# A fused decoder step: raw transposes of the first rows, their scale applied later, and the first weights in quarters

## The chip, the cores and the metric

One NeuronCore of one Trainium2 chip runs the whole program. The metric is the device time of one execution in microseconds (us); lower is better. The kernel before was timed three times: 1256.57, 1258.19 and 1259.11 us, median 1258.19 us.

## What is computed

One layer of a decoder on 264 rows of 1024 features (256 prompt rows, 8 decode rows), everything in float32. The part that the change touches is the start:

```python
def rms_norm(x, g):
    xf = x.astype(jnp.float32)
    y = xf * lax.rsqrt(jnp.mean(xf * xf, axis=-1, keepdims=True) + EPS)
    return (y * g.astype(jnp.float32)).astype(x.dtype)

parts = jnp.split(rms_norm(x, norm_attn) @ w_in, cuts, axis=-1)   # D_MODEL 1024 -> 4888 columns
q_a, k_c, v_c, k_s, v_s, k_w, v_w, g_nsa, q_b, k_b, v_b, g_mrg = parts
```

Then come QK-norm and rotary of queries and keys, a compression of cached and new keys and values (two small MLPs with GELU), two attentions (NSA and MoBA, for prompt and decode rows), a gated merge through `w_up_a`, `w_up_b` and `w_out`, and a mixture of 32 experts of 1024 x 2048 and 1024 x 1024 weights (12 MiB each, about 403 MB in all).

## The kernel before, in words

Every engine has its own instruction list, written out by hand in the order in which it runs; semaphores (`wait_ge`, `then_inc`) tie them together. There is no planner. All loads of weights go through SyncE's one DMA queue, in program order; some cache pages go through ScalarE's queue.

**The start.** SyncE (lines 2163 to 2179) issues, in this order: the first 128 prompt rows `x[:, 0]` (512 KB), the identity (64), the gains (4), the first half (4 of 8 chunks of 128 rows) of projection block 0 of `w_in` (1024), the second 128 prompt rows (512), the 8 decode rows (32), the second half of block 0 (1024), block 1 (1120), seven small gain vectors (32 each), the rest of the constants (1174), the page table, the four small loads of `small_weights` (line 494), and then blocks 2 to 5 (2048 KB each). `small_weights` begins with `sp.wait_ge(n_sq, 3)`: its destinations lie on ScalarE's `square_out`, so it waits until ScalarE has squared all three row tiles.

For each row tile i, ScalarE squares the rows with a running sum (line 2327) and takes the root (2329), VectorE takes the reciprocal (2428) and multiplies the rows by it (2429), TensorE transposes the scaled rows in eight pieces into a PSUM bank pair (`turn_x`, 2232), and ScalarE (2336) and VectorE (2437) copy the transposed rows out into `xnT`, times the feature gain. TensorE starts with eight matmuls on zeros (2227) while the first data comes.

**The projection.** `project(n)` (2243) runs blocks n = 0 to 5 of `w_in`: for each of the two prompt tiles eight chunk products of 128 x 512 into one bank, then the decode rows as 128 x 32 products. ScalarE's `evacuate(n)` (2339) copies each bank out and squares it for the QK-norm. Block 0 is special: `turn_x(1)` stands in the middle of its first tile and `turn_x(2)` after it. SyncE then issues, in order, its share of the compressed-cache pages (`cached`, 2152: 32 DMAs), the two 2 MB weights of the compression, stores of new keys, the key pages of three caches (`load_item` of items 8 to 10), and the stores and reloads of `q_rows` (2200 to 2204), by which the decode queries go out to HBM and come back on all partitions. VectorE's `moba_scores` (L985, L987) needs these.

**After the projection.** TensorE transposes the cached rows, runs the compression's hidden layer (L635), packs the result (`packed`, L687) and goes on to attention, where `gate_tile(f)` (L698) reads `xnT` again for the merge gates. `packed(1)` waits for the last GELU piece, which VectorE (L994 to L1006) and ScalarE (L888) make between and behind the eight `moba_scores`. GpSimd (`compress_pool`, 557) clears buffers. Then come the merge and the experts, whose weights stream through nine slots; a slot is loaded again as soon as its matmuls are done.

Of the kernel before, what the change touches and what calls it, by code (L numbers as in the profile page):

```python
# [26 lines left out]
P = 128  # L27
# [94 lines left out]
def build(nc, t, const_at, const_w):  # L122
    ctx = ExitStack()
    with ctx:
# [151 lines left out]
        x_in, gain_in, n_root, n_scaled, n_turned = [sem(f"n_x{i}") for i in range(NT)], sem("n_gain"), sem("n_root"), sem("n_scaled"), sem("n_turned")  # L276
        n_sq, n_kept, n_clear = sem("n_sq"), [sem(f"n_kept{i}") for i in range(NT)], sem("n_clear")
# [104 lines left out]
        cmp_read, cmp_ready, cmp_T, cmp_kept = sem("cmp_read"), sem("cmp_ready"), sem("cmp_T"), sem("cmp_kept")  # L382
# [4 lines left out]
        early, early_in = [at(out_at, 2 * D), at(d_at, 2 * D)], sem("early_in")  # L387
        extra, extra_in = at(extra_at, SLOT), x_in[1]
        odd_first, odd_second, odd_last = at(k_at, SLOT), at(d_at + KC * TOK, 3 * D), at(m_at + 2 * D, D)
# [25 lines left out]
        def landing(slot):  # L415
            base = dense_count[slot] if slot < RING else 16 if slot == EXTRA else 0
            return (early_in if slot == EARLY else extra_in if slot == EXTRA else ring_in[slot]), base, 16 * len(slot_runs(slot))
# [139 lines left out]
        def compress_pool(pool):  # L557
            pool.wait_ge(rope_done, 5)
            for i in range(2):
                nc.gpsimd.memset(rT[i][:, 18, :], 0.0).then_inc(n_clear, 1)  # L560
            pool.wait_ge(p_turned, 11)
# [129 lines left out]
        def gate_tile(pe, f):  # L691
            if f % 4 == 0:
# [8 lines left out]
        def attend_pe(pe):  # L701
# [66 lines left out]
            def unit_values(u):  # L768
# [3 lines left out]
                if u == 0:  # L772
                    pe.wait_ge(cmp_kept, 1)
# [1386 lines left out]
        with nc.Block() as block:  # L2160
            @block.sync
            def _(sp):
# [4 lines left out]
                sp.dma_start(first[:, 0:KC // 2, :], source[:, 0:KC // 2, :]).then_inc(half_in, 16)  # L2167
                sp.dma_start(x[:, 1, :], t["x_prompt"][0, P:2 * P, :]).then_inc(x_in[1], 16)
                sp.dma_start(x[0:DB, 2, :], t["x_sample"].rearrange("a b d -> (a b) d")).then_inc(x_in[2], 16)
                sp.dma_start(first[:, KC // 2:KC, :], source[:, KC // 2:KC, :]).then_inc(ring_in[0], 16)  # L2170
# [52 lines left out]
            def _(pe):  # L2223
                zeros = xdT.rearrange("p c b -> p (c b)")
                pe.wait_ge(n_clear, 2)
                for _ in range(8):
# [5 lines left out]
                def turn_x(i):  # L2232
                    r = ROWS[i]
                    pe.wait_ge(n_scaled, i + 1)
# [8 lines left out]
                def project(n, between=None):  # L2243
# [6 lines left out]
                    for i in range(2):  # L2250
# [11 lines left out]
                        for c in range(KC):  # L2262
                            if n == 0 and i == 0 and c == KC // 2:
                                turn_x(1)
                                pe.wait_ge(ring_in[0], landed[0])
                            mm = nc.tensor.matmul(out, xnT[:, c, P * i:P * i + P], columns(c), start=(c == 0), stop=(c == KC - 1))  # L2266
                        mm.then_inc(proj_done, 1)
                        if n == 0 and i == 0:
                            turn_x(2)
# [44 lines left out]
                project(V_B, lambda: turn(K_B))  # L2314
                compress_pe(pe)
# [5 lines left out]
            def _(act):  # L2321
                act.wait_ge(n_clear, 1)
                nc.scalar.activation(small[:, 12:13], eps, ACT.Sqrt)
                for i in range(NT):
# [3 lines left out]
                    act.wait_ge(n_sq, i + 1)  # L2328
                    nc.scalar.activation(rstd[0:r, i:i + 1], sumsq[0:r, i:i + 1], ACT.Sqrt, scale=1.0 / D, bias=eps[0:r, :]).then_inc(n_root, 1)
                    if i == 0:  # L2330
# [206 lines left out]
```

## Time and profile before

| | |
|---|---|
| median of three runs | 1258.19 us (1256.57 to 1259.11) |
| profiled execution, its own time | 1257.01 us |
| its span (first to last instruction) | 1255.1 us, 16432 instructions |
| busy: PE, DVE, ACT, POOL | 1214.9 us (97%), 379.0 (30%), 194.5 (15%), 16.1 (1%) |
| HBM read | 459.54 MB, 370 GB/s over the span |
| chain that ended last, shares | PE 58%, DMA 29%, SPq 8%, DVE 3%, issue 1% |
| DMA in 40 slices, GB/s, slices 1 to 12 | 326 187 245 240 213 200 126 161 347 308 233 419 |
| DMA, slices 13 to 39 | 424 to 431 |

PE is TensorE, DVE VectorE, ACT ScalarE, POOL GpSimd, SPq the issuing of DMAs by SyncE. A slice is 31.4 us. The span is cut short by 1.9 us against the execution's own time; differences in the span are differences in the time. In the chain, "SPq" is the time in which SyncE was issuing DMAs and nothing else is seen to have held up what came after.

### The profile page before, as it was taken

The numbers are of one execution on the slowest core, as the hardware profiler recorded it, in microseconds if no ns is written. First come the engines' busy times: TensorE is split into PE (matmuls) and PEld (weight loads), VectorE is DVE, ScalarE is ACT, GpSimd is POOL, SyncE is SP. The second block draws the span as 40 slices with busy tenths as digits, with TensorE's granted clock in tenths as the row PEclk, the third lists the DMA queues.
The fourth block names the chain that finished last, engine by engine and source line by source line (L and its number), as shares of the span: only waits on it lengthen the run. The fifth ranks groups of instructions, "written<-read, shape, count | busy, mean of one in ns | idle before, by whom it ended". The sixth has DMA issues, their size and how long they took to land.

```text
span 1255.1 us, 16432 instructions
## 1 busy us (share of the span) xinstructions
PE 1214.9 (97%) x6431; PEld 552.2 (44%) x6431; DVE 379.0 (30%) x931; ACT 194.5 (15%) x440; POOL 16.1 (1%) x28
## 2 busy tenths in 40 slices
PE   9999999999999999999999899999999898999998
PEld 5556777685533433334333232343334333333332
DVE  2545865324533221222222121321222121221223
ACT  3223244202301100010100001110010100000011
POOL 0000000011000000000000000000000000000000
PEclk9999999999999999999999999999999999999999
DMA  9787563598699999999999999999999999999995
GB/s 326 187 245 240 213 200 126 161 347 308 233 419 431 426 424 429 427 426 427 427 426 427 427 428 426 426 428 426 425 426 428 428 426 427 427 426 428 426 427 244
DMA packets 81067, 463.58 MB, mean 369 GB/s; under 512 B 20290, under 2 KB 35418, under 8 KB 55906
## 3 DMA queue, kind: packets, MB, share of 16 engines
q1 hardware_dynamic: 76386, 461.51, 90.8%
q10 hardware_dynamic: 4608, 1.05, 0.5%
q8 instruction: 52, 0.85, 0.3%
q14 instruction: 21, 0.17, 0.0%
HBM read 459.54 MB, written 5.09 MB: 370 GB/s over the span
## 4 chain that ended last, share of the span: by engine, by line
PE 58%; DMA 29%; SPq 8%; DVE 3%; issue 1%; ACT 0%; DVEq 0%
PE banks L1301 21%; DMA arena<-w_down 18%; PE banks L1381 10%; DMA arena<-w_gu 10%; PE banks L698 5%; PE banks L1278 3%; PE banks L1238 2%; PE banks L875 2%; PE banks L1567 2%; SPq L2157 2%; SPq L238 1%; PE banks L1259 1%; PE banks L1331 1%; SPq L265 1%; PE banks L1287 1%
## 5 line engine op out<-in xcount | busy, mean ns | idle before, releaser
L1301 PE MATMUL banks<-arena 128*64 128x512 f32 x1984 | 440.6, 594 | 19.3 <-DMA arena<-w_gu 18.4
L1301 PEld LDWEIGHTS banks<-arena 128*64 128x64 f32 x1984 | 134.8, 136 | 294.1 <-issue 248.8
L1381 PE MATMUL banks<-arena 128*64 128x512 f32 x992 | 221.2, 593 | 4.2 <-DMA arena<-w_down 3.8
L1481 DVE TENSOR_SCALAR arena<-banks 128x512 f32<-128x512 f32 x32 | 22.1, 692 | 373.3 <-PE banks L1301 352.9
L1381 PEld LDWEIGHTS banks<-arena 128*64 128x64 f32 x992 | 69.5, 137 | 137.3 <-issue 117.1
L1437 ACT ACTIVATE arena<-arena 128x512 f32<-128x512 f32 x32 | 20.2, 630 | 524.8 <-DVE arena L1481 524.8
L2266 PE MATMUL banks<-arena 128*128 128x512 f32 (+1 forms) x192 | 77.9, 562 | 1.0 <-DMA arena<-w_in 1.0
L1522 DVE TENSOR_TENSOR arena<-banks,arena 128x528 f32<-128x528 f32 x64 | 45.0, 707 | 76.6 <-PE banks L1278 76.6
L1238 PE MATMUL banks<-arena 128*64 128x512 f32 x256 | 61.2, 599 | 0.9 <-DVE arena L1474 0.9
L1432 DVE TENSOR_TENSOR arena<-banks,arena 128x512 f32<-128x512 f32 x33 | 22.8, 692 | 129.5 <-PE banks L1259 129.5
L698 PE MATMUL banks<-arena 128*128 128x264 f32 x256 | 59.9, 387 | 0.5 <-ACT arena L914 0.5
L1278 PE MATMUL banks<-arena 128*128 128x264 f32 (+1 forms) x256 | 59.7, 393 | 0.0
L1278 PEld LDWEIGHTS banks<-arena 128*128 128x128 f32 (+1 forms) x256 | 45.5, 189 | 20.5 <-issue 13.0
L1441 ACT COPY arena<-banks 128x512 f32<-128x512 f32 x32 | 18.7, 585 | 222.9 <-PE banks L1365 222.9
L2266 PEld LDWEIGHTS banks<-arena 128*128 128x128 f32 x192 | 35.8, 190 | 37.9 <-issue 35.3
L698 PEld LDWEIGHTS banks<-arena 128*128 128x128 f32 x256 | 47.4, 190 | 8.7 <-ACT arena L914 0.9
L1467 ACT COPY arena<-banks 64x512 f32<-64x512 f32 x64 | 37.1, 580 | 25.3 <-PE banks L1381 17.8
L635 PE MATMUL banks<-arena 128*128 128x285 f32 x128 | 32.1, 410 | 0.0
L1238 PEld LDWEIGHTS banks<-arena 128*64 128x64 f32 x256 | 16.7, 136 | 31.5 <-issue 30.3
L1259 PEld LDWEIGHTS banks<-arena 128*128 128x128 f32 x132 | 18.2, 205 | 26.8 <-issue 23.1
L1477 DVE CAST arena<-arena 96x64 bf16 (+1 forms) x32 | 6.0, 190 | 79.1 <-PE banks L1381 79.1
L875 PE MATMUL banks<-arena 128*128 128x264 f32 x128 | 28.9, 386 | 0.5 <-issue 0.5
(378 smaller groups left out, 934.4 us busy)
## 6 DMA issues: line engine op xcount, KB each, us to landing
arena<-w_gu SPq DMA_DIRECT2D x107, 2048.0 KB, 32.5
arena<-w_down SPq DMA_DIRECT2D x61, 2048.0 KB, 33.3
arena<-w_gu SPq DMA_DIRECT2D x21, 1536.0 KB, 29.6
arena<-w_in SPq DMA_DIRECT2D x8, 2048.0 KB, 14.3
arena<-w_gu SPq DMA_DIRECT2D x21, 512.0 KB, 32.1
arena<-w_down SPq DMA_DIRECT2D x5, 1024.0 KB, 26.8
arena<-cache_moba_k SPq DMA_DIRECT2D x16, 256.0 KB, 2.8
arena<-cache_moba_v SPq DMA_DIRECT2D x16, 256.0 KB, 2.9
```

Source lines behind the costliest of these rows:

```text
L635: mm = nc.tensor.matmul(banks[:, 4 + 2 * i + m, 0:19 * NC].rearrange("p (s c) -> p s c", c=NC), w1[:, r, P * m:P * m + P], rT[i][:, :, fir ...
L698: mm = nc.tensor.matmul(banks[:, B_GATE, 0:TOK], w[:, c, P * (f % 4):P * (f % 4) + P], xnT[:, c, :], start=(c == 0), stop=(c == KC - 1))
L875: mm = nc.tensor.matmul(banks[:, 4 + 2 * (m % 2) + x, 0:TOK], w[:, j, P * m:P * m + P], o[:, j, :], start=(j == 0), stop=(j == 3))
L1238: nc.tensor.matmul(banks[64 * x:64 * x + 64, BX, :], sel[:, i, :], h[:, i, 512 * x:512 * x + 512], start=(i == 0), stop=False, tile_positi ...
L1259: mm = nc.tensor.transpose(banks[:, BT, P * k:P * k + P], xg[:, first:first + 2 * P - 1:2], ident)
L1278: mm = nc.tensor.matmul(out[:, x, 0:TOK], y[rows, 512 * x + P * c:512 * x + P * c + P], selT[rows, :], start=True, stop=True)
L1301: mm = nc.tensor.matmul(banks[64 * x:64 * x + 64, BG + b, :], xgT[:, c % 4, 64 * (c // 4):64 * (c // 4) + 64], weights(slot, 2 * D * (c % ...
L1381: mm = nc.tensor.matmul(banks[64 * x:64 * x + 64, bank, :], product[:, c, 64 * part:64 * part + 64], weights(slot, D * c + 512 * x, 512), ...
L1467: nc.scalar.copy(y[64 * half:64 * half + 64, 512 * x:512 * x + 512], banks[64 * x:64 * x + 64, bank, :]).then_inc(S["ykept"], 1)
L1522: nc.vector.tensor_tensor(v, scatter_banks(c)[:, :, 0:TOK], v, ALU.add).then_inc(S["added"], 1)
L1567: mm = nc.tensor.matmul(banks[:, 2 * i + n, :], sig[:, c, P * i:P * i + P], slot((OUT_A, OUT_B)[c // 4], 4)[:, c % 4, 512 * n:512 * n + 51 ...
L2266: mm = nc.tensor.matmul(out, xnT[:, c, P * i:P * i + P], columns(c), start=(c == 0), stop=(c == KC - 1))
```

## The change

The prompt rows are transposed as they were loaded. Their factor `rstd` is left out of `xnT` and is applied per row when a projection bank is copied out (`scale=row_rstd`). The decode rows are still scaled before they are transposed. The gates read `xnT` transposed, with rows along the free axis, so `xnT` itself is multiplied by the factors later: VectorE spreads them on two diagonals (`scales_spread`), TensorE multiplies these by ones, ScalarE copies the bank to `scale_rows`, and GpSimd multiplies `xnT` by it in four pieces before the first `gate_tile`. Block 0 of `w_in` is loaded in four quarters, all before the second prompt rows and the decode rows. `turn_x(1)` moves from chunk 4 to chunk 7 of the first tile, `turn_x(2)` into the second tile; the matmuls on zeros go from 8 to 3. ScalarE's order becomes: copy out tile 0, root of tile 0, copy out tile 1, root of the decode rows, root of tile 1. `small_weights` and its wait are not touched.

```diff
@@ -274,6 +274,9 @@
+        quarter_in, third_in, row_scale, gate_rows_scaled = sem("early_in"), sem("cmp_kept"), gain_in, x_in[0]
+        CMP_KEPT = 16 + 1
+        SCALES_SPREAD, SCALES_SUMMED, SCALES_KEPT, ROWS_SCALED = 18, 19, 20, 16 + 4
@@ -379,13 +382,14 @@
-        cmp_read, cmp_ready, cmp_T, cmp_kept = sem("cmp_read"), sem("cmp_ready"), sem("cmp_T"), sem("cmp_kept")
+        cmp_read, cmp_ready, cmp_T, cmp_kept = sem("cmp_read"), sem("cmp_ready"), sem("cmp_T"), third_in
...
-        early, early_in = [at(out_at, 2 * D), at(d_at, 2 * D)], sem("early_in")
+        early, early_in = [at(out_at, 2 * D), at(d_at, 2 * D)], quarter_in
...
+        scales_spread, scale_rows = at(extra_at, 2, P), at(extra_at + 2 * P, 2 * P)
@@ -413,7 +417,7 @@
         def landing(slot):
-            base = dense_count[slot] if slot < RING else 16 if slot == EXTRA else 0
+            base = dense_count[slot] if slot < RING else 16 if slot in (EXTRA, EARLY) else 0
@@ -558,6 +562,11 @@
+            pool.wait_ge(proj_done, 18)
+            pool.wait_ge(row_scale, SCALES_KEPT)
+            for c in range(0, KC, 2):
+                rows = xnT[:, c:c + 2, 0:2 * P]
+                nc.gpsimd.tensor_tensor(rows, rows, scale_rows.unsqueeze(1).broadcast_to([P, 2, 2 * P]), ALU.mult).then_inc(gate_rows_scaled, 1)
@@ -689,6 +698,8 @@
         def gate_tile(pe, f):
+            if f == 0:
+                pe.wait_ge(gate_rows_scaled, ROWS_SCALED)
@@ -770,7 +781,7 @@
-                    pe.wait_ge(cmp_kept, 1)
+                    pe.wait_ge(cmp_kept, CMP_KEPT)
@@ -2164,10 +2175,12 @@
-                sp.dma_start(first[:, 0:KC // 2, :], source[:, 0:KC // 2, :]).then_inc(half_in, 16)
+                sp.dma_start(first[:, 0:2, :], source[:, 0:2, :]).then_inc(half_in, 16)
+                sp.dma_start(first[:, 2:4, :], source[:, 2:4, :]).then_inc(quarter_in, 16)
+                sp.dma_start(first[:, 4:6, :], source[:, 4:6, :]).then_inc(third_in, 16)
+                sp.dma_start(first[:, 6:KC, :], source[:, 6:KC, :]).then_inc(ring_in[0], 16)
...
-                sp.dma_start(first[:, KC // 2:KC, :], source[:, KC // 2:KC, :]).then_inc(ring_in[0], 16)
@@ -2223,7 +2236,7 @@
             def _(pe):
...
-                for _ in range(8):
+                for _ in range(3):
@@ -2231,7 +2244,10 @@
                 def turn_x(i):
...
-                    pe.wait_ge(n_scaled, i + 1)
+                    if i < 2:
+                        pe.wait_ge(x_in[i], 16)
+                    else:
+                        pe.wait_ge(n_scaled, 2)
...
                     for c in range(KC):
@@ -2260,13 +2276,18 @@
                         for c in range(KC):
-                            if n == 0 and i == 0 and c == KC // 2:
+                            if n == 0 and i == 0 and c == 2:
+                                pe.wait_ge(quarter_in, 16)
+                            if n == 0 and i == 0 and c == 4:
+                                pe.wait_ge(third_in, 16)
+                            if n == 0 and i == 0 and c == 6:
+                                pe.wait_ge(ring_in[0], landed[0])
+                            if n == 0 and i == 0 and c == 7:
...
-                                pe.wait_ge(ring_in[0], landed[0])
+                            if n == 0 and i == 1 and c == KC // 2:
+                                turn_x(2)
...
-                        if n == 0 and i == 0:
-                            turn_x(2)
@@ -2312,6 +2333,12 @@
+                pe.wait_ge(const_in, 16)
+                pe.wait_ge(row_scale, SCALES_SPREAD)
+                pe.wait_ge(p_copied, 10)
+                for i in range(2):
+                    mm = nc.tensor.matmul(banks[:, 7, P * i:P * i + P], ones, scales_spread[:, i, :], start=True, stop=True)
+                mm.then_inc(row_scale, 1)
@@ -2321,20 +2348,26 @@
             def _(act):
...
-                for i in range(NT):
+
+                def root_of(i, order):
...
-                    act.wait_ge(n_sq, i + 1)
+                    act.wait_ge(n_sq, order)
...
-                    if i == 0:
-                        act.wait_ge(gain_in, 17)
-                    if i != 1:
-                        k = i // 2
-                        act.wait_ge(n_turned, 2 * k + 2)
-                        for c in range(4):
-                            kept = nc.scalar.activation(xnT[:, c, P * k:P * k + P], banks[:, 2 * k, P * c:P * c + P], ACT.Copy, scale=gainT1[:, c:c + 1])
-                        kept.then_inc(n_kept[k], 1)
+
+                def keep_turned(k):
+                    act.wait_ge(n_turned, 2 * k + 2)
+                    for c in range(4):
+                        kept = nc.scalar.activation(xnT[:, c, P * k:P * k + P], banks[:, 2 * k, P * c:P * c + P], ACT.Copy, scale=gainT1[:, c:c + 1])
+                    kept.then_inc(n_kept[k], 1)
+
+                act.wait_ge(gain_in, 17)
+                keep_turned(0)
+                root_of(0, 1)
+                keep_turned(1)
+                root_of(2, 2)
+                root_of(1, 3)
...
                 def evacuate(n, between=None):
@@ -2346,12 +2379,14 @@
-                        src = banks[:, 2 * (n % 2) + i, 0:w]
+                        src, row_rstd = banks[:, 2 * (n % 2) + i, 0:w], rstd[:, i:i + 1]
+                        if n == 0:
+                            act.wait_ge(n_scaled, 2 * i + 1)
...
-                            nc.scalar.copy(v_moba[:, i, :], src).then_inc(tile_out, 1)
+                            nc.scalar.activation(v_moba[:, i, :], src, ACT.Copy, scale=row_rstd).then_inc(tile_out, 1)
...
-                        nc.scalar.copy(tiles(raw[n % 4], w)[:, i, :], src).then_inc(tile_out, 1)
-                        nc.scalar.activation(tiles(squares[n % 2], w)[:, i, :], src, ACT.Square).then_inc(tile_out, 1)
+                        nc.scalar.activation(tiles(raw[n % 4], w)[:, i, :], src, ACT.Copy, scale=row_rstd).then_inc(tile_out, 1)
+                        nc.scalar.activation(tiles(squares[n % 2], w)[:, i, :], src, ACT.Square, scale=row_rstd).then_inc(tile_out, 1)
@@ -2399,6 +2434,8 @@
+                act.wait_ge(row_scale, SCALES_SUMMED)
+                nc.scalar.copy(scale_rows, banks[:, 7, 0:2 * P]).then_inc(row_scale, 1)
@@ -2422,20 +2459,29 @@
             @block.vector
...
             def _(dve):
-                for i in range(NT):
-                    r = ROWS[i]
-                    dve.wait_ge(n_root, i + 1)
-                    settle(nc.vector.reciprocal(rstd[0:r, i:i + 1], rstd[0:r, i:i + 1]))
-                    nc.vector.tensor_scalar(x[0:r, i, :], x[0:r, i, :], rstd[0:r, i:i + 1], None, ALU.mult).then_inc(n_scaled, 1)
-                    if i == 0:
-                        dve.wait_ge(n_turned, 1)
-                        nc.vector.tensor_copy(gainT1, banks[:, 7, 256:256 + KC]).then_inc(gain_in, 1)
-                        dve.wait_ge(gain_in, 17)
-                    if i != 1:
-                        k = i // 2
-                        dve.wait_ge(n_turned, 2 * k + 3)
-                        nc.vector.tensor_tensor(xnT[:, 4:8, P * k:P * k + P], banks[:, 2 * k + 1, :].rearrange("p (c n) -> p c n", c=4),
-                                                gainT1[:, 4:8].unsqueeze(2).broadcast_to([P, 4, P]), ALU.mult).then_inc(n_kept[k], 1)
+
+                def keep_turned(k):
+                    dve.wait_ge(n_turned, 2 * k + 3)
+                    nc.vector.tensor_tensor(xnT[:, 4:8, P * k:P * k + P], banks[:, 2 * k + 1, :].rearrange("p (c n) -> p c n", c=4),
+                                            gainT1[:, 4:8].unsqueeze(2).broadcast_to([P, 4, P]), ALU.mult).then_inc(n_kept[k], 1)
+
+                dve.wait_ge(n_turned, 1)
+                nc.vector.tensor_copy(gainT1, banks[:, 7, 256:256 + KC]).then_inc(gain_in, 1)
+                dve.wait_ge(gain_in, 17)
+                keep_turned(0)
+                dve.wait_ge(n_root, 1)
+                nc.vector.reciprocal(rstd[:, 0:1], rstd[:, 0:1]).then_inc(n_scaled, 1)
+                keep_turned(1)
+                dve.wait_ge(n_root, 2)
+                settle(nc.vector.reciprocal(rstd[0:DB, 2:3], rstd[0:DB, 2:3]))
+                nc.vector.tensor_scalar(x[0:DB, 2, :], x[0:DB, 2, :], rstd[0:DB, 2:3], None, ALU.mult).then_inc(n_scaled, 1)
+                dve.wait_ge(n_root, 3)
+                nc.vector.reciprocal(rstd[:, 1:2], rstd[:, 1:2]).then_inc(n_scaled, 1)
+                dve.wait_ge(n_scaled, 3)
+                dve.wait_ge(ident_in, 16)
+                for i in range(2):
+                    last = nc.vector.tensor_scalar(scales_spread[:, i, :], ident, rstd[:, i:i + 1], None, ALU.mult)
+                last.then_inc(row_scale, 1)
```

## Rows read from the trace of the kernel before

**Rows 1.** TensorE's waits, whole span: for whom, us in total, times, longest.

```profile
PE banks L1301 <- DMA arena<-w_gu: 18.4, 17, 2.7
...
PE banks L687 <- DVE arena L1006: 0.8, 1, 0.8
```

**Rows 2.** Chain of waits, 100 to 150 us: start, length, what.

```profile
105.17 0.40 SPq L2202
106.26 2.53 DMA q_rows<-arena
...
109.72 6.25 DMA arena<-q_rows
116.09 1.24 DVE arena L985
...
145.97 0.44 ACT arena L888
...
147.09 1.59 PE banks L687 x16
```

**Rows 3.** SyncE's own waits, 0 to 160 us.

```profile
SPq L2195 <- DMA q_rows<-arena: 2.2, 1, 2.2
```

**Rows 4.** Chain of waits, 0 to 40 us, SyncE's issues.

```profile
14.23 0.34 SPq L497
...
17.43 0.66 SPq L238
...
19.78 5.15 SPq L238
```

**Rows 5.** Timeline of ScalarE, 4 to 20 us: start, length, instruction, [idle before <- releaser].

```profile
4.20 1.06 ACT L2327 ACTIVATE arena<-arena 128x1024 f32<-128x1024 f32 x1 [1.98 <-DMA arena<-x_prompt]
...
10.86 1.06 ACT L2327 ACTIVATE arena<-arena 128x1024 f32<-128x1024 f32 x1 [1.57 <-DMA arena<-x_prompt]
...
12.24 1.04 ACT L2327 ACTIVATE arena<-arena 8x1024 f32<-8x1024 f32 x1
...
14.07 1.14 ACT L2336 ACTIVATE arena<-banks,arena 128x128 f32<-128x128 f32 x4 [0.37 <-PE banks L2237]
```

**Rows 6.** Timeline of TensorE's products, 0 to 45 us.

```profile
1.11 6.19 PE L2227 MATMUL banks<-arena 128*128 128x256 f32 x16 [1.11 <-POOL arena L2410]
...
9.50 3.67 PE L2266 MATMUL banks<-arena 128*128 128x512 f32 x8 [1.02 <-DMA arena<-w_in]
13.38 1.09 PE L2237 MATMUL banks<-arena 128*128 128x128 f32 x8 [0.21 <-DVE arena L2429]
...
18.43 7.13 PE L2266 MATMUL banks<-arena 128*128 128x512 f32 x16
```

**Rows 7.** Line 2227, products of 2 to 3 and 6 to 7.3 us: ns min/median/max.

```profile
L2227 PE MATMUL banks<-arena x4: 634/634/634, 1.7 to 3.0; 128*128 128x256 f32 x4
...
L2227 PE MATMUL banks<-arena x6: 377/379/634, 5.5 to 6.9; 128*128 128x256 f32 x6
```

**Rows 8.** Windows: each engine's busy us, then granted clock, DMA share, GB/s.

```profile
0.00:2.00 2.00, 0.89 (x2) 0.80 (x3) 0.01 (x1) 1.28 (x1) 1.14 (x10) 1.00 0.14 29
0.00:3.60 3.60, 2.48 (x6) 2.04 (x7) 0.01 (x1) 1.49 (x2) 1.14 (x10) 1.00 0.49 160
0.00:14.80 14.80, 12.46 (x43) 8.33 (x44) 3.74 (x10) 7.57 (x18) 1.14 (x10) 1.00 0.88 298
14.80:20.00 5.20, 5.20 (x20) 2.51 (x19) 0.82 (x3) 1.50 (x4) 0.00 (x0) 1.00 0.80 279
```

**Rows 9.** DMAs issued near 13.0 and 17.4 us: KB, us to landing.

```profile
arena<-const SPq DMA_DIRECT2D x1, 1174.0 KB, 9.6
...
arena<-w_in SPq DMA_DIRECT2D x1, 2048.0 KB, 11.3
```

**Rows 10.** Timeline of ScalarE, 81 us.

```profile
81.95 0.58 ACT L2353 COPY arena<-banks 128x512 f32<-128x512 f32 x1 [10.30 <-DMA s_v_s<-arena]
```

**Rows 11.** Timeline of GpSimd, 26 us.

```profile
26.75 0.40 POOL L2417 COPY arena<-arena 128x256 f32<-128x256 f32 x1 [25.04 <-ACT arena L2354]
```

## The prediction

> **What bounds the kernel now.** I read TensorE's waits first. Over the whole span it waits for little: 18.4 us for expert weights, all in the second half, and next to nothing before [rows 1]. The page's row of DMA rates says why: from slice 13 on the queue moves 424 to 431 GB/s without a break, so in the experts the time is the stream's, and the stream begins when the part before it is through. What the front gains or loses then reaches the end one to one, if it gets that far. So I followed the chain of waits back from the middle. The row to find is TensorE's `packed(1)` at 147.09: it is released by the last GELU piece (ACT L888, then DVE L1006), and TensorE idled 0.8 us for it [rows 1, 2]. Behind that stands an unbroken run of VectorE from 116.09, begun when the reloaded `q_rows` landed; these were issued behind the store of `q_rows` (2.53 us), and that behind SyncE's issue at 105.17 [rows 2]. In SyncE's own waits this 2.2 us for the store is all it waits for until after the projection; it never waits for TensorE there [rows 3]. From 17.43 on its list is either blocked in the push of a big load, when the queue is full (5.15 us at 19.78), or simply issuing, one DMA behind the other, to 105.17 [rows 2, 4].
>
> So two chains run to 147 us: TensorE's, 0.8 us ahead, and SyncE's with VectorE behind it, which sets the time. The change works on the first. I have to ask what it does to the second.
>
> **Part by part: TensorE's front.** Before, the first half of block 0 holds the first product until 9.50 [rows 6]. By order in the queue, 1.64 MB had been asked for when it landed, and the second rows (2.17 MB) landed at 10.86 [rows 5]: 0.52 MB in 1.4 us, 0.37 MB per us. After, a quarter is 0.52 MB, so the quarters land near 8.0, 9.4, 10.8 and 12.2, and the second rows, now at 3.22 MB, near 13.7. The first rows land at 4.20 [rows 5] and need no square, root or multiply before they are turned; they are out of the banks by about 7. TensorE starts at 8.0 instead of 9.5. Each chunk product is two records, and eight records take 3.67 us (sixteen, the second tile: 7.13), so 0.43 us a record and 0.86 a chunk once they follow each other [rows 6]. Seven chunks from 8.0: 14.0, with no wait for a quarter. Then `turn_x(1)` for 0.9 us, chunk 7 to 15.8, the second tile with `turn_x(2)` inside to 23.2. Before, that tile ended at 18.43 + 7.07 = 25.5 [rows 6]. TensorE gains 2.3 us, at full rate.
>
> That rate is not certain. The zeros' products took 634 ns each at 2 to 3 us and 377 ns at 6 to 7 us, though the column of the granted clock says 1.00 in both [rows 7, 8]; I read the durations as the two levels, 1.2 and 2.4 GHz. They ran without a gap from 1.11 to 7.3 [rows 6]. Five of eight are taken away, so this work ends near 3.7, and then come a gap, transposes of 1 to 2 us, and a gap to 8.0. If the engine is still at the low level at 8.0 and rises near 12, it loses half of 4 us: seven chunks end at 15.9, and the gain shrinks to 0.4 us. I take this case (6 in 10), because the work ahead of 8.0 is broken where it was whole. The Trainium skill, "TensorE: Matmul & The Clock Gate", What's actually happening, has the slow state as the default and activity as what releases it; by that rule the early gaps speak for the slow case, and rows 7 agree that the start was slow.
>
> **SyncE's list, which the change does not edit.** `small_weights` waits for three squares. Before, the third was done at about 13.4 (12.24 + 1.04 and the read of the sum) [rows 5], and SyncE came there at 14.23 and went straight on [rows 4]. After, ScalarE's third square is that of tile 1, behind `keep_turned(1)` and the decode rows. `keep_turned(1)` starts 0.7 us after `turn_x(1)` begins (13.38 to 14.07), takes 1.14, one square to the next is 1.38 (10.86 to 12.24), and the last takes 1.2: 4.4 us in all [rows 5, 6]. From 14.0 that is 18.4; from 15.9, 20.3. SyncE stands still for 4.2 or 6.1 us, and everything queued behind goes with it: the four small loads (14.23 to 17.43, so 3.2 us; 2.3 if their longer pushes were a full queue) [rows 4] and then blocks 2 to 5, 8 MB. Block 2 is issued at 20.7 to 21.6, or 22.6 to 23.5, instead of 17.43.
>
> How much of this is hidden by loads already queued? The windows give 4.41 MB moved by 14.8 and 5.86 MB by 20.0 [rows 8]. What is ahead of the small loads, the constants included, sums to 5.83 MB. So on average the 16 engines have nothing left at 20.0. The constants landed at 13.02 + 9.6 = 22.6 [rows 9], 2.6 us later. That is part notice of completion and part the slowest of the 16 engines. The first rows are 0.52 MB; at 3.6 us that much had moved, and they landed at 4.20 [rows 5, 8]. If that 0.6 us is all the notice costs, the slowest engine works until 22.0 and loses little. If all of 2.6 is notice, every engine is idle from 20.0. A new load begins to move about 1.1 us after its issue: of the first, issued at 0.72, 0.06 MB had moved by 2.0 [rows 8]. Block 2 then begins at 21.8 to 22.7 at the high clock, or 23.7 to 24.6 at the low. Idle queue, against 20.0 or 22.0: 0 to 2.7 us, or 1.7 to 4.6 us. I take the middles: 1.3 and 3.2 us. The Trainium skill, "DMA: Bandwidth & Descriptors", Anatomy of one DMA, puts some 2 us of fixed cost on each DMA, most of it the receipt of the write; by that rule every engine is out of work at 20.6, and the low-clock sum would be 24.2 - 20.6 = 3.6 us. The first rows' 0.6 us speaks against it, the constants' 2.6 for it.
>
> The blocked pushes, as at 19.78, end when the queue has drained so far, so they move with the queue and give nothing back; behind them SyncE is bound by its own issuing. Hence 105.17 becomes 108.4, and 147.09 becomes 150.3. Blocks 2 to 5 still come in time: block 2 landed at 17.43 + 11.3 = 28.7 [rows 9] and is needed at 36.6 or earlier by 2.3.
>
> **What it does elsewhere.** Two more issues of 0.45 us lie under the full queue. Scaling in the bank copies is free: ScalarE's scaled copies of 128x128 take 0.29 us each [rows 5]. After block 5: two products and a ScalarE copy, 0.65 us on TensorE. Its new waits there (constants, spread factors, p_copied 10) and at the first gate tile stand ahead of the whole compression and the merge, but what they wait for is done before TensorE comes: the constants by 22.6, the factors by about 21, the copy of Q_B and K_B's second bank just behind `turn(K_B)`. GpSimd: four operations of 128x512 with two inputs. A one-input 128x256 copy took 0.40 us [rows 11]; 0.8 to 2 us each, done by 116 at worst, and the first gate tile comes at 159. Nothing. The wait of `evacuate(K_B)` for the stores of K_CMP already held ScalarE until 81.95 [rows 10]; these stores move with SyncE's list, so ScalarE will hold TensorE by about 1 us at the turn of Q_B, which comes out of TensorE's lead. That lead, 0.8 + 0.4 - 0.65 + 3.2 us, becomes idle time before 147 us (at the high clock 0.8 + 2.3 - 0.65 + 1.3), 3.7 us at most.
>
> **The sum.** Nothing of TensorE's gain arrives; the shift of SyncE's chain does: +3.2 us. Against the profiled execution's 1257.01 that is 1260.2. The runs' median, 1258.19, lies 1.2 above it, so 1261.4 us.
>
> **The rivals.** First, the gain goes through: -2.3 us, 1255.9. It needs `packed(1)` to be ready earlier, so a queue that loses nothing and a chain through `q_rows` that is not the last. Against it: the 0.8 us wait, the run of VectorE, and that nothing in SyncE's list gets shorter. 1 in 10, for what I misread. Second, the stall stays under the queue: the high clock comes early and the slowest engine has work until 22. Then 0 to +1.7, near 1258.9. For it: after an idle 1.02 us before 9.50 the products still took 0.43 us a record [rows 6]. 3.3 in 10. Third, the idle time before 147 lets the clock fall: what follows then runs at half rate for some microseconds, as the products of rows 7 did until about 5.5; 4 us of that cost 2, on top of 3.2: 1263.4. The trace has no idle of that length to read it from. 1 in 10. The Trainium skill's page on the clock gate, HAM oscillation, names this as a cost of idle gaps, with the clock back at half. The forecast holds the rest, 4.7 in 10, with its own range 1259.9 to 1263.0.
>
> **How the numbers follow.** A measurement of this kernel can tell about 0.2%, 2.5 us. The forecast lies just past it: two thirds of its chance (0.31) and the third rival (0.10) are slower, the rest of it (0.16) and most of the second (0.31) within; the first is faster but for a part. Faster 0.09, same 0.49, slower 0.42. The range takes in all of the second rival and the third: 1256.8 to 1264.4.
>
> **What would show it.** Right: SyncE's L497 near 18 to 20 us with a wait for ScalarE, block 2 behind it, DMA share well under 1 near 20 to 24; `q_rows` stored at 106.5 to 110; TensorE through block 0 earlier but idle some 3 to 5 us before the second L687, at 148 to 151. Products of 0.86 us a record until about 12 us show the low clock. Wrong: L687 before 147, or a full queue through 20 to 24 us.

## The result, and the profile after

The changed kernel takes 1266.83 us (median of 12 executions, 1257.57 to 1270.08) against 1256.82 for the kernel before (12, 1256.30 to 1259.25). The ratio is 1.0056 with the interval 1.0041 to 1.0072 (the two medians alone stand at 1.0080): slower, clear of the noise and by more than I had said, though under 1% of the whole. The executions of the changed kernel are of two kinds: three lie at 1257.57 to 1259.71, nine at 1263.89 to 1270.08, and the mean granted clock is 0.999 in the first three and 0.990 to 0.997 in the others. The profile shown is one of the nine: 1269.84 us, 12.8 above the profiled execution before, and its span of 1268.0 us is 12.9 above.

SyncE's list first, 12 to 42 us (start, length, instruction):

```profile
12.61 0.29 SPq L2188 DMA_DIRECT2D arena<-page_table  x1
20.78 0.34 SPq L501 DMA_DIRECT2D arena<-cmp_pos_k  x1
...
22.59 10.88 SPq L238 DMA_DIRECT2D arena<-w_in  x4
```

L501 is `small_weights`, L497 before the change: issued at 14.23 before [rows 4], now at 20.78, and block 2 at 22.59 instead of 17.43. SyncE's own waits (for whom, us in total, times, longest) give the reason, and ScalarE's timeline the work that it waited for:

```profile
SPq L501 <- ACT arena L2355: 7.9, 1, 7.9
```

```profile
17.24 1.14 ACT L2362 ACTIVATE arena<-banks,arena 128x128 f32<-128x128 f32 x4 [8.78 <-PE banks L2253]
18.26 1.04 ACT L2355 ACTIVATE arena<-arena 8x1024 f32<-8x1024 f32 x1
...
19.62 1.04 ACT L2355 ACTIVATE arena<-arena 128x1024 f32<-128x1024 f32 x1
20.57 0.19 ACT L2355 ACTIVATION_READ_ACCUMULATOR arena<-arena 128x1 f32 x1
```

The third square ends at 20.76 and SyncE goes on at 20.78. Meanwhile the DMA queue runs dry (windows: length, busy us of PE, PEld, DVE, ACT, POOL, granted clock, DMA share, GB/s):

```profile
18.00:20.00 2.00, 2.00 (x6) 0.85 (x5) 0.59 (x3) 1.97 (x6) 0.00 (x0) 1.00 0.60 254
20.00:22.00 2.00, 2.00 (x5) 0.59 (x4) 1.33 (x4) 1.97 (x5) 0.00 (x0) 1.00 0.03 9
22.00:24.00 2.00, 2.00 (x12) 1.25 (x12) 0.65 (x4) 0.24 (x1) 0.00 (x0) 1.00 0.51 89
...
147.00:150.00 3.00, 0.68 (x9) 0.47 (x7) 2.40 (x7) 1.26 (x3) 0.00 (x0) 1.00 1.04 394
150.00:153.00 3.00, 3.00 (x20) 2.74 (x17) 1.74 (x6) 0.92 (x1) 0.00 (x0) 0.50 1.05 395
153.00:172.00 19.00, 19.00 (x120) 14.12 (x119) 7.79 (x35) 5.24 (x15) 0.53 (x1) 0.50 0.90 308
172.00:176.00 4.00, 4.00 (x15) 3.13 (x13) 3.72 (x21) 1.36 (x6) 0.00 (x0) 0.76 0.62 178
```

In the kernel before, the queue stayed full there:

```profile
18.00:22.00 4.00, 4.00 (x17) 2.06 (x17) 0.36 (x2) 1.03 (x2) 0.00 (x0) 1.00 1.01 364
```

The lower windows hold the second finding: from 150 to about 174 us TensorE's granted clock is 0.50, that is 1.2 GHz. Its timeline there:

```profile
144.58 1.61 PE L696 MATMUL banks<-arena 128*15 128x64 f32 x16
146.03 1.48 PE L658 MATMUL banks<-arena 128*128 128x128 f32 x12
149.83 2.66 PE L696 MATMUL banks<-arena 128*15 128x64 f32 x16 [2.32 <-DVE arena L1017]
...
170.98 5.26 PE L709 MATMUL banks<-arena 128*128 128x264 f32 x16
176.72 3.83 PE L709 MATMUL banks<-arena 128*128 128x264 f32 x16 [0.48 <-ACT arena L925]
```

L696 is `packed` (L687 before), L709 the products of `gate_tile` (L698 before). The kernel before has `packed(0)` and the first gate tile at

```profile
143.41 1.61 PE L687 MATMUL banks<-arena 128*15 128x64 f32 x16
...
159.06 3.83 PE L698 MATMUL banks<-arena 128*128 128x264 f32 x16
```

Sixteen products of the same shape take 1.61 us before the gap of 2.32 us and 2.66 after it. From `packed(1)` to the first gate tile it is 21.15 us, against 11.97 before (147.09 to 159.06); the first tile itself takes 5.26 against 3.83. So of the 12.9 us, 2.7 are the later start of `packed(1)` and about 10 the half clock behind it. The chain in between is the forecast one (chain of waits: start, length, what):

```profile
109.15 0.40 SPq L2215
110.24 2.02 DMA q_rows<-arena
...
112.72 0.43 SPq L2210
113.19 5.62 DMA arena<-q_rows
118.94 1.24 DVE arena L996
...
148.72 0.44 ACT arena L899
149.83 2.66 PE banks L696 x16
```

Each stands 2.7 to 4.0 us later than in [rows 2]. The experts are as before: TensorE's wait for `w_gu` is 18.0 us [rows 1: 18.4]. At the start, TensorE's timeline is

```profile
1.12 2.93 PE L2240 MATMUL banks<-arena 128*128 128x256 f32 x6 [1.12 <-POOL arena L2447]
4.57 0.24 PE L2243 MATMUL banks<-arena 8*128 8x8 f32 x1 [0.52 <-DMA arena<-const]
4.74 1.97 PE L2253 MATMUL banks<-arena 128*128 128x128 f32 x8
7.56 9.20 PE L2289 MATMUL banks<-arena 128*128 128x512 f32 x14 [0.86 <-DVE arena L2465]
16.60 1.04 PE L2253 MATMUL banks<-arena 128*128 128x128 f32 x8
...
26.29 1.95 PE L2306 MATMUL banks<-arena 128*32 128x128 f32 x64
```

Seven chunks take 9.20 us at first: the groups by line show 1061 ns a record from 8.6 to 12.0 us and 592 from 13.6 on (a record lasts longer than the distance to the next, which is some 0.86 and 0.45 us):

```profile
L2289 PE MATMUL banks<-arena x5: 1061/1061/1061, 8.6 to 12.0; 128*128 128x512 f32 x5
```

Block 0's decode products begin at 26.29, 0.8 us later than before.

### The profile page after: what moved, and what is told of

It is laid out like the page before. It is cut to its first block, busy times and chain, and to the rows that moved or that the text cites. A ratio compares the mean times of both kernels' runs of the same rounds, so it can differ in the third digit from the quotient of the medians.

```text
span 1268.0 us, 16435 instructions
## 1 busy us (share of the span) xinstructions
PE 1227.0 (97%) x6425; PEld 559.5 (44%) x6425; DVE 379.4 (30%) x931; ACT 196.5 (15%) x441; POOL 21.1 (2%) x32
## 4 chain that ended last, share of the span: by engine, by line
PE 63%; DMA 28%; SPq 4%; DVE 3%; issue 1%; ACT 0%; DVEq 0%
PE banks L1312 21%; DMA arena<-w_down 18%; PE banks L1392 10%; DMA arena<-w_gu 10%; PE banks L709 5%; PE banks L2289 4%; PE banks L1289 3%; PE banks L1249 2%; PE banks L886 2%; PE banks L1578 2%; PE banks L1270 1%; PE banks L1342 1%; SPq L265 1%; PE banks L1298 1%; PE banks L762 1%
## 5 line engine op out<-in xcount | busy, mean ns | idle before, releaser
L2289 PE MATMUL banks<-arena 128*128 128x512 f32 (+1 forms) x192 | 81.1, 579 | 0.9 <-DVE arena L2465 0.9
L709 PE MATMUL banks<-arena 128*128 128x264 f32 x256 | 61.4, 394 | 0.5 <-ACT arena L925 0.5
L1289 PEld LDWEIGHTS banks<-arena 128*128 128x128 f32 (+1 forms) x256 | 45.5, 189 | 20.5 <-issue 13.0
L709 PEld LDWEIGHTS banks<-arena 128*128 128x128 f32 x256 | 48.4, 194 | 9.4 <-ACT arena L925 0.9
```

What stands on the lines that cost most here:

```text
L709: mm = nc.tensor.matmul(banks[:, B_GATE, 0:TOK], w[:, c, P * (f % 4):P * (f % 4) + P], xnT[:, c, :], start=(c == 0), stop=(c == KC - 1))
L1289: mm = nc.tensor.matmul(out[:, x, 0:TOK], y[rows, 512 * x + P * c:512 * x + P * c + P], selT[rows, :], start=True, stop=True)
```

## The experiments

Each is timed against the kernel before on the same chip, 11 or 12 executions against 29 to 35. "Late" below counts executions of 1263 us and more. My theory: the wait of `small_weights` shifts SyncE's list and so `packed(1)`, and the idle time ahead of it lets the clock fall. The rivals: TensorE's slow start does it; the new scaling work does it.

**e1: the squares ahead of the second copying out.**

```diff
                 root_of(0, 1)
-                keep_turned(1)
                 root_of(2, 2)
                 root_of(1, 3)
+                keep_turned(1)
```

> The changed kernel with one thing else: ScalarE takes the squares and roots of the decode rows and of tile 1 before it copies tile 1 out of the banks, not after. TensorE's work is not touched. Theory (SyncE's wait for the third square delays blocks 2 to 5, the whole queue list and so the second L696; TensorE's idle time in front of it lets its clock fall): the third square is done near 15, SyncE's first small load goes out there and not at 20.8, the queue stays full, and the second L696 stands again at 147.1 +- 0.6 instead of 149.8. TensorE's idle time in front of it is then 1 to 2.5 us, more than the 0.75 us of the kernel before, since TensorE comes earlier; if the clock falls all the same, about 1266 us, if not, about 1257 us. Rival (the added scaling work on ScalarE, VectorE and GpSimd delays the second L696, the wait is harmless): it stays at 149.8 and the time at 1266.

1259.11 us (1256.65 to 1260.81) against 1257.71, ratio 1.0009 (1.0000 to 1.0018), none late. SyncE's issues, a window, and `packed(1)`:

```profile
15.57 0.34 SPq L501 DMA_DIRECT2D arena<-cmp_pos_k  x1
...
17.61 11.00 SPq L238 DMA_DIRECT2D arena<-w_in  x4
```

```profile
20.00:22.00 2.00, 2.00 (x10) 0.76 (x9) 0.00 (x0) 0.00 (x0) 0.00 (x0) 1.00 1.05 381
```

```profile
147.82 1.59 PE L696 MATMUL banks<-arena 128*15 128x64 f32 x16 [0.73 <-DVE arena L1017]
```

With the order of three ScalarE steps alone, the queue stays full and the 10.0 us between the medians shrink to 1.4. `packed(1)` is 0.1 us later than I had allowed, and the gap is smaller: TensorE reached `packed(0)` only at 144.16, so its own chain set `packed(1)`. TensorE's slow start is still there (14 records in 8.74 us), and so is all the scaling. Neither costs the 10 us by itself.

**e2: keep the late chain, fill the gap.** Five products of 128x256 into an unused bank between the last keys' transposes and `packed(1)`.

```diff
             pe.wait_ge(const_in, 16)
+            for _ in range(5):
+                nc.tensor.matmul(banks[:, 5, 0:256], ident, cst[:, P:P + 256], start=True, stop=True)
```

> The changed kernel with five products of 128x256 into an unused bank between the last turn_keys(3) and the second packed(), 2.1 us of work on TensorE in the time in which it waits there. Their result is read by nobody. Theory (of the 12.9 us by which the span grew, 2.7 are SyncE's later list and 10.2 are the clock at half from 150 to 173 us, which TensorE's idle time in front of L696 brings): the granted clock stays at 1.00, the second L696 stays at 149.8 to 150.3, and the time is 1256.8 + 3.0 = about 1260 us in all runs, without the spread from 1257.6 to 1270. Rival (the clock falls for another reason, such as the small products before, or the DMA load that begins at 147): it falls as before, 1266 to 1270 us.

1259.18 us (1255.77 to 1261.35), ratio 1.0011 (1.0002 to 1.0020), none late.

```profile
144.61 2.32 PE L719 MATMUL banks<-arena 128*128 128x256 f32 x10
147.03 1.59 PE L696 MATMUL banks<-arena 128*15 128x64 f32 x16
```

```profile
150.00:173.00 23.00, 22.28 (x175) 17.96 (x173) 15.77 (x75) 9.56 (x32) 0.53 (x1) 1.00 0.88 302
```

Added work takes the changed kernel from 1266.83 to 1259.18 us: the half clock is the larger part of the loss, and without the gap no execution is late. In the profiled execution TensorE also had its full rate early, so this profile alone would not do; the eleven times do.

**e3: both.** The edits of e1 and e2 together.

> Both edits of the two kernels before it in this series: the roots first, and the five idle-time products. Theory: nothing is left of the loss; second L696 at 147.1 to 147.6 and clock at 1.00: 1256.8 to 1257.5 us, the same as the kernel before within 0.1%. Rival (something else of the change costs time further on): above 1258.5.

1260.88 us (1257.39 to 1262.74), ratio 1.0021 (1.0013 to 1.0030), none late. A miss: where there is no gap, the fillers stand in the way. They ended at 149.5, and `packed(1)` began at 149.51 instead of 147.8. The clock fell here too, later and with TensorE busy:

```profile
160.00:162.00 2.00, 2.00 (x22) 2.00 (x22) 0.60 (x5) 0.10 (x2) 0.00 (x0) 0.55 1.05 389
162.00:164.00 2.00, 2.00 (x7) 1.15 (x4) 1.97 (x11) 1.12 (x5) 0.00 (x0) 0.50 1.10 373
```

**e4: the late wait alone, in the kernel before.**

```diff
             sp.wait_ge(n_sq, 3)
+            sp.wait_ge(tile_out, 2)
```

> The kernel before with one wait more: SyncE's small_weights also waits until the first projection tile is copied out and squared (19.0 us instead of passing at 14.2), so SyncE's list stands still for some 4.8 us and nothing else is touched. Theory: the queue runs dry near 20, the second L687 moves from 147.1 by 1.5 to 3 us, TensorE idles 2.2 to 3.8 us before it, and the clock falls in most executions: 1264 to 1270 us, in the others 1259. Rival (the queue covers the delay; the loss of the changed kernel comes from its other edits): 1256.8.

1260.33 us (1258.01 to 1267.47), ratio 1.0035 (1.0018 to 1.0052), three of eleven late, at 1266.04 to 1267.47.

```profile
19.05 0.34 SPq L498 DMA_DIRECT2D arena<-cmp_pos_k  x1
...
147.92 1.70 PE L688 MATMUL banks<-arena 128*15 128x64 f32 x16 [1.67 <-DVE arena L1007]
```

```profile
148.00:150.00 2.00, 2.00 (x19) 1.89 (x19) 1.71 (x6) 1.01 (x1) 0.00 (x0) 0.82 1.05 410
150.00:152.00 2.00, 2.00 (x19) 0.67 (x17) 1.15 (x4) 0.21 (x1) 0.00 (x0) 0.50 1.06 393
152.00:154.00 2.00, 2.00 (x23) 1.69 (x20) 0.65 (x6) 0.59 (x1) 0.00 (x0) 0.83 1.06 388
```

Nothing of the change but a later issue of the small loads, and both steps are there: later by 0.8 us, a gap of 1.67, and the clock down behind it, here for 3.4 us. Both are smaller than I had expected (1.5 to 3 us, a gap of 2.2 to 3.8, most executions late), and the profiled execution (1259.13 us) is not one of the three late ones.

**e5: a warm start.** The changed kernel with five matmuls on zeros instead of three, and two more after `turn_x(0)`.

```diff
-                for _ in range(3):
+                for _ in range(5):
...
                 turn_x(0)
+                for _ in range(2):
+                    nc.tensor.matmul(banks[:, 5, 0:256], zeros[:, 0:P], zeros, start=True, stop=True)
```

> The changed kernel with more work on zeros at the start: five products before the identity is there (the kernel has three) and two more behind turn_x(0), so that TensorE works almost without a gap from 1.1 us to the first chunk product. Theory (in the changed kernel TensorE is at 1.2 GHz until about 13 us because its early work is broken; a product record took 1.06 us and not 0.59): the records come down to 0.59 us before 8 us, block 0's first decode product starts near 23.5 instead of 26.3, the third square is done near 18 and the small loads go out there, so the second L696 moves from 149.8 to 148 to 148.8. TensorE then idles even longer before it, 3 us, and the clock falls there: 1264 to 1268 us. Rival (idle time before L696 is not what makes the clock fall): 1256 to 1259.

1257.98 us (1255.49 to 1267.93) against 1257.91, ratio 1.0012 (0.9990 to 1.0034), two late (1266.64, 1267.93). The seven chunks now take 6.28 us instead of 9.20 and block 0's decode products start at 23.52, so the third square comes sooner too:

```profile
7.71 6.28 PE L2291 MATMUL banks<-arena 128*128 128x512 f32 x14
...
146.75 1.59 PE L696 MATMUL banks<-arena 128*15 128x64 f32 x16 [1.92 <-DVE arena L1017]
```

I had expected most executions late, as SyncE still waits 5.1 us, and `packed(1)` at 148 to 148.8. The gap was 1.92 us, near that of the changed kernel, yet only two of eleven were late, and in the profile the clock stayed at 1.00 until 159.1. A gap is not enough by itself.

The median is as good as with e1, so the slow start has its part in the loss after all: it makes the third square later (SyncE waits 7.9 us with it, 5.1 without), and of each such delay the queue covered a part. Block 2 was issued 2.4, 3.4 and 5.2 us late in e5, e4 and the changed kernel; the stores of `q_rows` were late by 0.9, 2.2 and 4.0 us, and `packed(1)` by -0.3, 0.8 and 2.7.

**e6, e7: take `q_rows` out of SyncE's shadow.** Stores and first reloads of `q_rows` one block earlier, in the kernel before (e6) and the changed one (e7).

```diff
-                    if n == 5:
+                    if n == 3:
+                        sp.wait_ge(rope_done, Q_B + 1)
...
+                    if n == 4:
                         sp.wait_ge(q_stored, 64)
...
                     load_item(sp, n + RING)
-                    if n == 4:
-                        sp.wait_ge(rope_done, Q_B + 1)
...
```

> The kernel before; SyncE stores the decode queries (q_rows) before it loads item 9 and fetches the first three pairs back before it loads item 10, some 10 us earlier in its list; nothing else is touched. Theory (SyncE's list, q_rows and VectorE's moba_scores set the second L687, TensorE's own work does not): VectorE begins its scores when its copies end, at 112 instead of 116.1, TensorE no longer waits before the second L687, which starts at 146.3: 0.7 us less, 1256 to 1257.3 us against 1257.7 (median of the runs before). Rival (TensorE's list sets it): 147.1 and no change. If the gain is more than 1 us, part of it is a clock that no longer dips in 148 to 170 us.

> The changed kernel with the same move of q_rows, and SyncE's late small loads left as they are. Theory: the chain through q_rows gets 4 us of room, more than the 2.7 it lost, so the second L696 is set by TensorE's own work, 147.5 us in executions with the low clock at the start and 145 in those without; no idle time in front of it, no fall of the clock there: 1255.5 to 1258.5 us. Rival (the late blocks 2 to 5 cost time in another way than through q_rows): above 1260.

e6: 1258.40 us (1256.12 to 1259.69), ratio 1.0000 (0.9991 to 1.0009). VectorE begins its scores at 110.74 instead of 116.09 and nothing comes of it, for it now waits for TensorE, and `packed(1)` still has its small wait (it stands 1.0 us earlier than before because in this execution TensorE was 1.0 us earlier at `packed(0)`, 142.41):

```profile
134.14 0.51 DVE L994 TENSOR_SCALAR arena<-banks 128x270 f32<-128x270 f32 x1 [0.84 <-PE banks L635]
```

```profile
146.07 1.59 PE L687 MATMUL banks<-arena 128*15 128x64 f32 x16 [0.73 <-DVE arena L1006]
```

e7: 1256.17 us (1254.67 to 1260.77), ratio 0.9991 (0.9979 to 1.0003), none late. SyncE still waits 7.2 us for the third square, and `packed(1)` begins at 148.28 with a gap of 0.73. That is later than the 147.5 I had expected, but without a longer gap. The 10 us between the medians are gone though `small_weights` is nearly as late as ever: its harm went by way of `q_rows`.

**e8, e9: which of them pay together.** e9 is e5's and e7's edits, e8 has e1's as well.

> The changed kernel with three of the edits together: roots before the second copy-out, work on zeros in the gaps of the start, q_rows early. Theory: block 0 is through 2.3 us earlier than in the kernel before, nothing holds TensorE before the second L696, which starts at 144.5 to 145.3 instead of 147.1: 1254.5 to 1256 us, faster than both kernels. Rival (the freed time goes into another wait, the hold of evacuate(K_B) on the stores of K_CMP or the DMA queue in the experts): 1257 or more.

> The changed kernel with the work on zeros at the start and q_rows early, its roots in the order of the change. Theory (the roots-first order held back the second copy-out and with it TensorE by 1 us in the kernel with all three, since the second rows' squares end near 16): block 0's first decode product starts at 23.5 (24.75 there), TensorE's own chain sets the second L696 at 145.3 to 145.8, 1.4 us before the kernel before: 1254 to 1256 us against some 1257.5. Rival (the lead is taken by the hold on the stores of K_CMP, which are late with SyncE's small loads): L696 at 146.5 or later, 1257.

e8: 1257.66 us (1255.87 to 1259.15) against 1257.91, ratio 0.9991 (0.9975 to 1.0007). A miss: `packed(1)` came at 146.70, not at 144.5 to 145.3. With the squares first, TensorE waits 0.84 us for the second rows to leave the banks. e9: 1256.35 us (1254.86 to 1259.38) against 1258.07, ratio 0.9983 (0.9970 to 0.9997), none late, the only version faster than the kernel before beyond its interval. Block 0's decode products start at 24.12 and `packed(1)` at

```profile
146.43 1.59 PE L696 MATMUL banks<-arena 128*15 128x64 f32 x16 [0.73 <-DVE arena L1017]
```

The time is in the range I had given, the position is not (145.3 to 145.8). e7 and e9 differ by less than their intervals.

**e10, e11: `small_weights` behind blocks 2 to 5**, added to e9 (e10) and alone in the changed kernel (e11).

```diff
-                small_weights(sp)
                 for n in range(2, RING):
                     load_item(sp, n)
+                small_weights(sp)
```

> The same with small_weights moved behind the loads of blocks 2 to 5, so that its wait for the third square holds back nothing. Theory: SyncE issues block 2 at 13, the queue never runs dry, the K_CMP stores and all that follows are where they were in the kernel before or earlier; TensorE sets the end of the dense part with no hold at the turn of Q_B: second L696 at 145.0 to 145.5, 1253.5 to 1255.5 us. Rival: as the kernel without this move, so that the late loads cost nothing once q_rows is early.

> The changed kernel with only small_weights moved behind blocks 2 to 5: the loss undone by another edit than the order of the roots, and without any change to ScalarE. Theory: the third square is as late as in the changed kernel (20.6 us), but nothing waits behind it; the second L696 stands at 147.0 to 148.2, set by TensorE's own chain where the clock was low at the start; 1257 to 1259.5 us against 1266.8. Rival (the ScalarE order was what the roots-first kernel repaired): 1264 or more.

e11: 1260.47 us (1258.02 to 1267.15) against 1258.07, ratio 1.0017 (0.9997 to 1.0036), one late; `packed(1)` at 147.87 with a gap of 0.72. It is a second way to undo the stall, and again most of the loss goes, if not quite as much as I had expected (1257 to 1259.5). e10: 1258.48 us (1256.40 to 1262.11), ratio 1.0002 (0.9987 to 1.0017), a miss: the small loads are now pushed behind 8 MB, from 28.83 to 37 us, and SyncE comes to its cache pages at 38.27 instead of 32.38 in e9. ScalarE's hold at the stores of K_CMP ends at 84.19 instead of 83.46, and TensorE waits 1.69 us for it instead of 0.57.

```profile
13.16 15.62 SPq L238 DMA_DIRECT2D arena<-w_in  x4
28.83 5.92 SPq L501 DMA_DIRECT2D arena<-cmp_pos_k  x1
```

The gap ahead of `packed(1)` in each profiled execution (that of the others isn't known), and the late ones among all:

| kernel | gap, us | late |
|---|---|---|
| changed | 2.32 | 9 of 12 |
| e4 | 1.67 | 3 of 11 |
| e5 | 1.92 | 2 of 11 |
| e1, e6, e7, e8, e9, e10 | 0.73 | 0 of 69 |
| e2, e3 (filled) | under 0.1 | 0 of 23 |
| e11 | 0.72 | 1 of 12 |
| before | 0.8 | 4 of 110 |

## Why the prediction was right or wrong

**The sign and the path: right.** The time was to be lost in `small_weights`, not in anything the change edits. Undoing that in two ways (e1, e11), doing only that (e4) and going round it (e7) each bear it out.

**TensorE's front: the slow case right, its size wrong.** Products at 1061 ns a record until nearly 13 us; block 0 ends 0.8 us later, where I had it 0.4 earlier. I had the low clock cost 2 us, from 8 to 12. Seven chunks took 9.20 us, and 6.28 in e5, where the zeros' products fill the start, so it cost 2.9, from the first product at 7.56 until 13 or so.

**SyncE's list: right.** Third square 20.3 forecast, 20.76 found; block 2 at 22.6 to 23.5 forecast, 22.59 found; the DMA share 0.03 over 20 to 22 us. The constants' 2.6 us were not all notice: in the changed kernel the engines were as good as idle from 20.0 (share 0.05 to 20.5, then 0.00), and the constants, issued at 12.13, landed 9.0 us later, at 21.1. So about 1.1 us is notice; what the other 1.5 before the change were, with loads queued behind, isn't shown.

**The shift to `packed(1)`: right in kind.** 3.2 us forecast, 2.7 found, and in part by two errors that cancel. The stores of `q_rows` were 4.0 us late, where I had 3.2, but their landing and reload, which I had left as they were, were faster by 1.1 (2.02 and 5.62 against 2.53 and 6.25).

**"TensorE's, 0.8 us ahead": wrong.** The 0.8 us wait was not a lead. In e6, with VectorE's scores 5 us earlier, it is 0.73, and 0.72 to 0.73 in seven kernels. It is the time of the last GELU piece behind TensorE's own last product; VectorE's run only happened to be as long. `packed(1)` follows `packed(0)` by 3.66 us where TensorE's chain sets it (e6) and by 3.68 before. The two chains were level, so each would have passed on any loss, and no gain of one alone would have arrived. This also explains why the gap became 2.3 us and not the 3 to 5 forecast: TensorE was itself 1.17 us late at `packed(0)` (144.58 against 143.41).

**The fall of the clock: the step that failed, by its size.** "4 us of that cost 2, on top of 3.2", 1 in 10. In the profile it lasted 24 us and cost about 10, and nine of twelve executions were late. The median is therefore 1266.83, above my range. The three executions without it (by their mean clock) average 1258.8, within it, and nearer the second rival than my forecast. In part that is the base: I had added the shift to a level of 1258.19, and twelve executions give 1256.82, so they are 2.0 us slower where I had 3.2. I mis-sized it because I priced the return by the dense products at the start, which are back at full rate after some 4 us. Behind `packed(1)` stand some 140 small products, 1 to 256 columns wide, and the clock came back only after the gate tile's wide products had begun at 170.98, though by the profile TensorE was busy 19.00 of 19.00 us from 153 to 172. In e4's profile it was back among the same small products after 3.4 us: so their size alone does not hold it down.

The Trainium skill, "TensorE: Matmul & The Clock Gate", HAM oscillation, has idle gaps between groups of products drop the clock to half, at a cost per gap. I took it for a small rival. The runs agree on the gap as a trigger (14 of 34 executions late in kernels whose profile has a gap of 1.67 us or more, 5 of 214 without), and only in part: e3's clock fell with no idle time ahead of it, which the rule doesn't give.

**The scaling: right.** Scaled bank copies take 0.69 us against 0.58, not free, but ScalarE has the time. GpSimd's four operations take 1.25 us each, within the 0.8 to 2, and end at 112.8. ScalarE's hold at the stores of K_CMP moved from 81.95 to 85.28, but TensorE, itself later, waited only 0.24 us at the turn of Q_B, as before, and not the 1 us that I had put down. e9 keeps all of this and is not slower than before.

**Open.** Why e5 was late in two executions and the changed kernel in nine, at gaps of 1.9 and 2.3 us, isn't settled; nor what brings the clock back after 3.4 us in one execution and 24 in another, nor what makes a few executions of the kernel before late. Only one late execution was profiled. That the others are late by the same half clock is inferred from their mean granted clock: 0.990 to 0.993 over 1266 us is 18 to 25 us at half clock, somewhere in the execution (short falls come among the experts too: the mean over 1100 to 1112 us is 0.86 in e4's profile). One of the nine (1263.89 us, 0.997) doesn't fit that. The changed kernel was timed in one batch and not again beside e1 to e11, which ran on three chips; that part of its nine in twelve belongs to its chip isn't excluded. The evidence on one chip is e4's 3 of 11 against none of 68 in e1, e2, e3 and the kernel before.

## What to carry to other kernels

When work on one engine is put in another order, look up every counter of it that another queue waits for, above all the DMA queue: here a wait in unedited code cost more than the edit could bring. A short wait ahead of a join isn't slack until one has checked that it isn't simply the latency of the last step. A gap of 2.3 us in TensorE's work, followed by small products, cost four times its length in one execution here; ahead of such a stretch a few filler products pay where the engine would be idle, and stand in the way where it would not (e3).

## What the runs showed of the hardware

- The clock can fall to 1.2 GHz without idle time ahead of it. In e9 TensorE was busy 12.03 of 13 us from 144 to 157 (the longest idle stretch, 0.73 us, lay 10.7 us back), and from 157 to 163 its granted clock was 0.50 to 0.53. The same happened in e1, e3, e5, e6 and e11, between 158.6 and 160.2 us, in the last small products before the first gate tile or the first products of that tile. It came back by itself after 3.4 us in e1, e5, e6 and e11 and 6.8 in e3 and e9.
- The granted clock's record is not to be trusted in the first microseconds: in the changed kernel it is 1.00 while the products took 1061 ns, and still 1.00 when they took 592. The Trainium skill, "TensorE: Matmul & The Clock Gate", Seeing it yourself, calls single records of the clock unreliable, and the trace agrees; the durations settle it.
- Where loads are already queued, SyncE's push of the next one can hold SyncE up: 15.62 us for four blocks of 2 MB in e10, and 5.92 for the first small load behind them, where it took 0.33 in e9. A small load that is moved behind big ones moves everything behind it as well, here the first cache page from 32.38 to 38.27.
